# Decay rows of the state space heads through a scratch tensor in device memory, products in pairs, three of four causal blocks, folded norms

## The reference

```python
def hybrid_layer(...):
    h = rms_norm(x, norm1_w); proj = h @ w_in
    q, k, v, z, xbc, dt_raw = split(proj)
    q, k = rms_norm(q), rms_norm(k)                # 8 heads of 128
    attn = moba_attention(q, k, v)                 # 256 positions are one block: plain causal attention
    xs, bm, cm = split(silu(causal_dwconv(xbc)))
    y = ssd_chunked_scan(xs, softplus(dt_raw + dt_bias), -exp(a_log), bm, cm)   # 16 heads of 64
    y = rms_norm((y + d_skip * xs) * silu(z))      # 2 groups of 512 channels
    x = x + concat([attn, y]) @ w_out
    return x + (silu(u_gate) * u_val) @ w_down     # feed-forward, 5632 wide, with a convolution
def hybrid_layer_2(...):
    # modulation by c @ w_ada, dilated attention of 8 heads, retention of 4 heads in two directions
    o = o * rsqrt(mean(o * o) + eps)               # over the 256 channels of each retention head
```

## Time and profile before

| | us |
|---|---|
| time, median of 3 runs | 1633.7 (1627.95 to 1634.38) |
| the profiled execution's own time | 1634.53 |
| its span, first to last instruction | 1632.9 |
| PE busy with matmuls | 1586.1 (97%) |
| PE loading weights (overlaps) | 1557.8 (95%) |
| DVE busy | 1161.2 (71%) |
| ACT busy | 812.0 (50%) |
| mean granted PE clock | 0.990 |

### The profile page before, as it was taken

How to read it: one execution, slowest core, us unless ns; L and a number is a source line. 1 busy time by engine, 2 the same in 40 slices (tenths; PEclk the granted TensorE clock), 3 DMA queues, 4 the chain that set the end, 5 groups by cost and what they waited for, 6 DMA issues and landing times.

```text
span 1632.9 us, 33515 instructions
## 1 busy us (share of the span) xinstructions
PE 1586.1 (97%) x13230; PEld 1557.8 (95%) x13230; DVE 1161.2 (71%) x1359; ACT 812.0 (50%) x985; POOL 28.6 (2%) x54
## 2 busy tenths in 40 slices
PE   7999999999999999999999999999799999999998
PEld 7998899989999999999999999999799999999997
DVE  7676677775778888888888888666674554664754
ACT  6445355544564544545445454444455644445553
POOL 0000000000000000000000000000000000000000
PEclk9999999999999999999999999999989999999998
DMA  9453344455559777787777875555455555455451
GB/s 348 140 180 130 129 144 153 146 191 181 183 181 346 272 267 285 262 314 261 264 298 267 304 272 199 190 180 187 135 194 194 194 194 173 137 171 172 162 155 78
DMA packets 85186, 336.15 MB, mean 206 GB/s; under 512 B 9456, under 2 KB 9712, under 8 KB 78704
## 3 DMA queue, kind: packets, MB, share of 16 engines
q1 hardware_dynamic: 77328, 281.05, 50.2%
q0 software_dynamic: 7056, 51.38, 8.6%
q10 hardware_dynamic: 720, 2.52, 0.4%
HBM read 332.82 MB, written 2.10 MB: 205 GB/s over the span
## 4 chain that ended last, share of the span: by engine, by line
PE 72%; DVE 4%; issue 2%; ACT 1%; POOLq 0%; DVEq 0%; ACTq 0%
PE PS L1182 23%; PE PS L1184 23%; PE PS L1186 23%; DVE ada_w L996 1%; DVE wlo L627 1%; ACT whi L273 1%; PE PS L1317 1%; DVE UV L950 1%; PE PS L1284 1%; PE PS L1463 0%; PE PS L1303 0%; DVE X L643 0%; PE PS L1453 0%; PE PS L1471 0%; PE PS L1227 0%
## 5 line engine op out<-in xcount | busy, mean ns | idle before, releaser
L1182 PE MATMUL PS<-gh,whi 128*128 128x256 f32 x3504 | 992.4, 283 | 12.2 <-DVE wlo L627 10.4
L1184 PE MATMUL PS<-gl,whi 128*128 128x256 f32 x3504 | 977.9, 279 | 0.0
L1186 PE MATMUL PS<-gh,wlo 128*128 128x256 f32 x3504 | 977.6, 279 | 0.0
L627 DVE TENSOR_TENSOR wlo<-raw,whi 128x1024 fp32r<-128x1024 f32 x528 | 643.9, 1223 | 405.9 <-ACT whi L273 404.9
L273 ACT ACTIVATE whi<-raw 128x1024 fp32r<-128x1024 f32 x528 | 556.9, 1059 | 697.8 <-PE PS L1186 695.2
L1182 PEld LDWEIGHTS PS<-gh,whi 128*128 128x128 f32 x3504 | 663.5, 189 | 19.5 <-issue 17.4
L1184 PEld LDWEIGHTS PS<-gl,whi 128*128 128x128 f32 x3504 | 662.5, 189 | 2.8 <-issue 1.9
L1186 PEld LDWEIGHTS PS<-gh,wlo 128*128 128x128 f32 x3504 | 664.5, 190 | 0.0
L1182 PE MATMUL PS<-ah,whi 128*128 128x256 f32 x688 | 194.5, 283 | 10.8 <-DVE UV L950 7.2
L1184 PE MATMUL PS<-al,whi 128*128 128x256 f32 x688 | 193.0, 281 | 0.0
L1186 PE MATMUL PS<-ah,wlo 128*128 128x256 f32 x688 | 192.9, 280 | 0.0
(11 more groups left out here) (212 smaller groups left out, 845.6 us busy)
## 6 DMA issues: line engine op xcount, KB each, us to landing
raw<-weights SPq DMA_DIRECT2D x528, 512.0 KB, 3.5
ada_w<-w_ada POOLq DMA_DIRECT2D x48, 1024.0 KB, 5.9
outT<-X SPq DMA_DIRECT2D x4, 512.0 KB, 2.8
X<-xT SPq DMA_DIRECT2D x3, 512.0 KB, 8.7
c<-const ACTq DMA_DIRECT2D x1, 1536.0 KB, 7.1
c_act<-c_rows POOLq DMA_DIRECT2D x1, 1024.0 KB, 9.8
X<-xT SPq DMA_DIRECT2D x2, 256.0 KB, 5.2
prm<-params ACTq DMA_DIRECT2D x1, 276.5 KB, 4.6
```

Of the source, the lines that this page charges most:

```text
L627: dve.tensor_tensor(wlo[:, j % SPLIT, :], raw[:, j, :], whi[:, j % SPLIT, :].bitcast(F32), ALU.subtract).then_inc(s_lo, 1)
L1182: pe.matmul(out[:, t, :], whi[:, b, w], hi[:, kt, :], start=first and half == 0 and (apart or t % 2 == 0), stop=False, skip_group_check=True)
L1184: pe.matmul(out[:, t, :], whi[:, b, w], lo[:, kt, :], start=False, stop=False, skip_group_check=True)
L1186: mm = pe.matmul(out[:, t, :], wlo[:, b, w], hi[:, kt, :], start=False, stop=last and half == 1, skip_group_check=True)
```

## The change

Decay rows go through device memory. ACT writes three copies of the rows to `ACUM`, POOL stores them to a scratch tensor `rows` (16 x 384), waits, and loads them back to every partition (128 x 6144 floats, 3.1 MB) into a full-size `EM`, which lies where `ada_w` and `c_act` will be; so `c_act` is now loaded after the first projection:

```diff
         def _(pool):
-            pool.wait_ge(s_gh, DT)
+            pool.wait_ge(s_at, 2)
+            pool.dma_start(rows, ACUM[...]).then_inc(s_rows, 16)
+            pool.wait_ge(s_rows, 16)
+            pool.dma_start(EM[...], rows.rearrange("h l -> (h l)").unsqueeze(0).to_broadcast([P, SSM_HEADS * 3 * P])
+                           ).then_inc(s_r, 16)
+            pool.wait_ge(s_evac, G_OUT + 2)
             pool.dma_start(c_act[:, :], c_rows).then_inc(s_crow, 16)
-            pool.wait_ge(s_evac, G_OUT + 2)
# ACT
                 if n == 19:
-                    act.activation(small[0:16, 256:512], PS[0:16, 7, S:2 * S], ACT.Copy).then_inc(s_at, 1)
+                    act.activation(ACUM[:, 0:2, :], PS[0:16, 7, S:2 * S]..., ACT.Copy).then_inc(s_at, 1)
+                    act.activation(ACUM[:, 2, :], PS[0:16, 7, S + P:2 * S], ACT.Copy).then_inc(s_at, 1)
-                if n == 32:
+                if n == IN_SLOTS + 27:
                     act.activation(c_act[:, :], c_act[:, :], ACT.Silu).then_inc(s_c, 1)
-                if 35 <= n < 35 + SSM_HEADS:
+                if 35 <= n < 35 + SSM_HEADS and n % 2:
+                    j = (n - 35) // 2
+                    act.wait_ge(s_e, 6 * j + 6)
+                    act.activation(EM[:, 2 * j:2 * j + 2, :, :], EM[:, 2 * j:2 * j + 2, :, :], ACT.Exp)
```

DVE's `decay(h)` stays in slot 34+h, but works in place in `EM`; the exponential and `weigh` now take two heads at once, in the slot of the second one's `decay`. PE drops the 16 row matmuls and takes two heads in every second slot:

```diff
             def decay(h):
-                dve.wait_ge(s_r, h + 1)
                 if h == 0:
+                    dve.wait_ge(s_r, 16)
-                    dve.tensor_scalar(EM[:, h % 3, k, :], PS[:, 4 + h % 2, lo:lo + P], NB[:, k, h:h + 1], 0.0, ...)
+                    dve.tensor_scalar(EM[:, h, k, :], EM[:, h, k, :], NB[:, k, h:h + 1], 0.0, ...)
+            def weigh(j):
+                dve.wait_ge(s_ex, j + 1)
+                pair = EM[:, 2 * j:2 * j + 2, :, :]
+                dve.tensor_tensor(pair, pair, CB[:, j // 4, :, :].unsqueeze(1).to_broadcast([P, 2, 3, P]), ALU.mult)
-                if 35 <= n < 35 + SSM_HEADS:
-                    weigh(n - 35)
+                if 35 <= n < 35 + SSM_HEADS and n % 2:
+                    weigh((n - 35) // 2)
# PE
-                if 34 <= n < 34 + SSM_HEADS:
-                    pe.matmul(PS[:, 4 + h % 2, 0:S], ident[0:16, h:h + 1].to_broadcast([16, P]), small[0:16, 256:512], ...)
-                if 37 <= n < 37 + SSM_HEADS:      # one head: two matmuls, 256 and 128 columns
+                if 37 <= n < 37 + SSM_HEADS and n % 2:
+                    j = (n - 37) // 2
+                    pe.wait_ge(s_m, j + 1)
+                    for c in range(2):
+                        for q in (2 * j, 2 * j + 1):
+                            lo = 64 * (q % 2)
+                            out = PS[lo:lo + 64, 6 + j % 2, P * c:S]
+                            em = EM[:, q, 0:2, :] if c == 0 else EM[:, q, 2, :]
+                            mm = pe.matmul(out, XD[:, c, 64 * q:64 * q + 64], em, start=(c == 0), stop=(c == 1), ...)
+                    mm.then_inc(s_y, 1)
```

The sums for the norms are folded on DVE first; the state space norm moves one slot later on PE, ACT and DVE:

```diff
-                if n in (56, 57):
-                    ssm_norm(n - 56)
+                if n in (54, 55):
+                    dve.wait_ge(s_ysq, n - 53)
+                    y = SQY[n - 54]
+                    link(dve.tensor_tensor(y[:, 0:2, :], y[:, 0:2, :], y[:, 2:4, :], ALU.add))
+                    dve.tensor_tensor(y[:, 0, :], y[:, 0, :], y[:, 1, :], ALU.add).then_inc(s_yf, 1)
+                if n in (57, 58):
+                    ssm_norm(n - 57)
# PE, state space norm: 4 matmuls a group at n = 55, 56 become 1 at n = 56, 57
-                    for t in range(4):
-                        mm = pe.matmul(PS[:, 6 + g, 0:S], ones, SQY[g][:, t, :], start=(t == 0), stop=(t == 3))
+                    pe.matmul(PS[:, 6 + g, 0:S], ones, SQY[g][:, 0, :], start=True, stop=True).then_inc(s_ysum, 1)
# retention, layer 2: DVE adds the two tiles at step 3, PE sums one at step 5
+                        dve.tensor_tensor(both[:, 0, :], both[:, 0, :], both[:, 1, :], ALU.add).then_inc(s_rf, 1)
```

Attention of layer 1 leaves the masked block out everywhere: scores of 128 and 256 columns in place of 2 x 256, scale and mask over 384 in place of 512, the maximum as two instructions (128 and 256) in place of one over 512, exponential and division over 128 and 256, three transposes in place of four, a copy of 384, and 256 and 128 columns with v:

```diff
-                        mm = pe.matmul(PS[:, 4, S * c:S * c + S], q[:, P * c:P * c + P], k, start=True, stop=True)
+                        at, keys = (S * c, S) if layer else (P * c, P + P * c)
+                        mm = pe.matmul(PS[:, 4, at:at + keys], q[:, P * c:P * c + P], k[:, 0:keys], start=True, stop=True)
+                        for b in range(2 if layer else c + 1):     # transposes
+                        first = 0 if layer else P * b
+                        mm = pe.matmul(PS[:, 6, first:S], VS[:, h % 2, b, :], PTS[:, h % 2, b, 0:S - first], ...)
```

More of the change, by code:

```diff
@@ L75, with build @@
 ADA_STEP = 6
-def build(nc, xT, weights, w_dt, w_ada, c_rows, params, const1, const2, outT):
+def build(nc, xT, weights, w_dt, w_ada, c_rows, params, const1, const2, rows, outT):
     ctx = ExitStack()
@@ L120, in build @@
         U, o = place("U", [P, 12, S + 3], offset=o)
-        mask, o = place("mask", [P, 2, S], offset=o)
+        mask, o = place("mask", [P, 3 * P], offset=o)
         conv_acc, _ = place("conv_acc", [P, 4, S], offset=o)
@@ L126, in build @@
         assert o <= nc.sbuf_usable_end, (o, nc.sbuf_usable_end)
+        EM, e = place("EM", [P, SSM_HEADS, 3, P], offset=ada_at)
+        assert e <= area
+        ACUM, _ = place("ACUM", [SSM_HEADS, 3, P], offset=area + 1024 * Q0)
         SQX1, _ = place("SQX1", [P, 2, 4, S], offset=area + 1024 * Q0)
@@ L175, in spread, with seen @@
             return PS[:, 2 * late_par[k - 2] + 1, 0:S]
+        def seen(h, c):
+            flat = SB1[:, h % 2, :, :].rearrange("p c d -> p (c d)")
+            return flat[:, P:3 * P] if c else flat[:, 0:P]
         def acc_tiles(par):
@@ L379, in attention @@
                         k = 2 * (h % 2) + b
-                        act.activation(SB[:, h % 2, b, :], SB[:, h % 2, b, :], ACT.Exp, bias=small[:, k:k + 1],
+                        rows = SB[:, h % 2, b, :] if layer else seen(h, b)
+                        act.activation(rows, rows, ACT.Exp, bias=small[:, k:k + 1],
                                        accum_out=small[:, 4 + k:5 + k]).then_inc(s_exp, 1)
@@ L385, in attention @@
                         act.wait_ge(s_pv, H - 1)
[L386 to L387 removed]
+                    if layer:
+                        act.activation(PTS[:, h % 2, :, :], PS[:, 5, :].rearrange("p (c d) -> p c d", c=2),
+                                       ACT.Copy).then_inc(s_pts, 1)
+                    else:
+                        act.activation(PTS[:, h % 2, :, :].rearrange("p c d -> p (c d)")[:, 0:3 * P], PS[:, 5, 0:3 * P],
+                                       ACT.Copy).then_inc(s_pts, 1)
                 if step == 5 and layer == 0:
@@ L853, in attention @@
                     for b in range(2):
-                        dve.tensor_scalar(SB[:, h % 2, b, :], SB[:, h % 2, b, :], small[:, 8 + k + b:9 + k + b], None,
-                                          ALU.mult).then_inc(s_pn, 1)
+                        rows = SB[:, h % 2, b, :] if layer else seen(h, b)
+                        dve.tensor_scalar(rows, rows, small[:, 8 + k + b:9 + k + b], None, ALU.mult).then_inc(s_pn, 1)
                 if step == 5 and layer:
@@ L1120, in slot2 @@
                         retained(r)
+                    if step == 3:
+                        dve.wait_ge(s_rsq, r + 1)
+                        both = SQR[:, r % 2, :, :]
+                        dve.tensor_tensor(both[:, 0, :], both[:, 0, :], both[:, 1, :], ALU.add).then_inc(s_rf, 1)
                     if step == 5:
@@ L1316, in attention @@
                     for b in range(2):
-                        mm = pe.matmul(PS[:, 6, 0:S], VS[:, h % 2, b, :], PTS[:, h % 2, b, :],
+                        first = 0 if layer else P * b
+                        mm = pe.matmul(PS[:, 6, first:S], VS[:, h % 2, b, :], PTS[:, h % 2, b, 0:S - first],
                                        start=(b == 0), stop=(b == 1))
@@ L1370, in slot1 @@
                     pe.matmul(PS[:, 6 + g, S:S + P], bm[:, P:S], cm[:, P:S], start=True, stop=True).then_inc(s_cb, 1)
-                if 34 <= n < 34 + SSM_HEADS:
-                    h = n - 34
-                    pe.wait_ge(s_xd, 16)
-                    if h >= 2:
-                        pe.wait_ge(s_e, 3 * h - 3)
-                    pe.matmul(PS[:, 4 + h % 2, 0:S], ident[0:16, h:h + 1].to_broadcast([16, P]), small[0:16, 256:512],
-                              start=True, stop=True).then_inc(s_r, 1)
@@ L1466, in slot2 @@
                     if step == 5:
-                        pe.wait_ge(s_rsq, r + 1)
+                        pe.wait_ge(s_rf, r + 1)
                         if r:
                             pe.wait_ge(s_rrt, r)
-                        for e in range(2):
-                            mm = pe.matmul(PS[:, 7, 0:S], ones, SQR[:, r % 2, e, :], start=(e == 0), stop=(e == 1))
-                        mm.then_inc(s_rsum, 1)
+                        pe.matmul(PS[:, 7, 0:S], ones, SQR[:, r % 2, 0, :], start=True, stop=True).then_inc(s_rsum, 1)
```

84 lines of the change are left out of this document (42 added, 42 removed).

## The result

| | before | changed |
|---|---|---|
| median, us (runs) | 1630.83 (1624.9 to 1634.38, 4) | 1602.41 (1599.52 to 1610.16, 4) |
| ratio, 95% interval | | 0.9836 [0.9803, 0.9868] |
| profiled execution, its span | 1634.53, 1632.9 | 1599.52, 1597.9 |
| mean granted clock | 0.990 | 0.988 |

By the ratio the change is worth 1.64%, or 26.8 us of 1630.8 (21.5 to 32.1); the two medians are 28.4 apart. The direction was forecast, the size was not: 1616 was the forecast, and the time lies 3.6 us under the lower end of the range. The two profiled executions are 35.0 us apart because the one of before took longer than all four of its timed runs and the one of after was the fastest of its four.

What follows compares the result with a forecast made beforehand. PE was taken as the bound, busy 1586.1 of 1632.9 us. Streaming gains of 22.0 less 1.6, 1.5, 0.3 and 0.4 made 18.2 us, so 1634.5 - 18.2 = 1616.3 us; range 1606 to 1628.

Steps and rivals of the forecast that it cites:

- Rows, 10.7: Slots 34 to 49: removing the row matmuls from PE's path gains 10.7 us, with the replacing transfer hidden.
- Head products in pairs, 2.7: State space heads: 8 pairs at 1.64 us, 13.1 in place of 15.8, gain 2.7; bounds gain 7.9 to loss 1.3.
- Rival 1: Head product pairs: the two column halves overlap, a pair costs 0.99, 5.2 us more gained, time 1612; chance 20%.
- Folds and the masked block, 8.6: Norm sums, attention scores, products with v and transposes: fewer or shorter PE instructions gain 8.6 us; covering DVE adds cost 0.
- the pace was an unknown of its own: All PE stretches: matmuls run at 0.1175 or 0.1132 us, cause unknown; 7 us allowed either way.
- Given back, 3.8: Slots 34 to 91: longer waits and clock loss give back 1.6, 1.5, 0.3 and 0.4 us.
- The half clock behind slot 68, 1.5: After slot 68's transposes wait 2.9 us, PE's clock falls to 1.2 in place of 2.4 GHz, losing 1.5 us.
- Losses in slots 87 to 91: Same DVE chain as before, PE comes 0.2 us earlier to it: 0.3 us lost.
- The base: Forecast subtracted from the profiled execution's 1634.5 us, 0.8 above the median of the runs it used.
- 2, the pace turns: Long PE stretches: 100 to 150 us more run at the slow pace, giving 1625 us; chance 15%.
- 3, DVE piles up: Slots 34 to 70: larger delay and late weight splits cost 3 to 7 us more, giving 1621; chance 10%.
- 4, the broadcast is late: Row load to all partitions: gain gone if it takes over 62 us; 1676 us at 30 GB/s; chance 5%.

Runs made afterwards that it cites:

- e10: Kernel before, with only the decay rows stored and read back to all partitions in place of their matmuls: 1624.36 us, ratio 0.9925 to the kernel before.
- e3: Changed kernel with the 16 row matmuls back on PE, without store and broadcast: 1613.93 us, ratio 0.9887 to the kernel before.
- e4: Changed kernel without the folds of the state space and retention norms: 1611.80 us, ratio 0.9861 to the kernel before.
- e5: Changed kernel with all four blocks of layer 1's attention computed again, the masked one included: 1610.60 us, ratio 0.9876 to the kernel before.
- e8: Changed kernel, unaltered, timed and profiled again: 1602.89 us, ratio 0.9829 to the kernel before.
- e1: Changed kernel with the four matmuls of a pair ordered head by head: 1609.66 us, ratio 0.9842 to the kernel before.
- e6: Changed kernel with the state space norm a slot earlier, folds kept where they were: 1598.65 us, ratio 0.9832 to the kernel before.

## Why the prediction was wrong

The forecast was 1616.3 and the median 1602.4, 13.9 us lower. By stretches, in us gained:

| units | forecast | measured | what it holds |
|---|---|---|---|
| 33 to 60 | 15.6 | 20.65 | rows, pairs, the state space norm |
| 60 to 98 | 0.9 | 2.97 | attention, less waits and clock |
| 98 to 127 | 0 | 3.27 | nothing that was changed but the last product with v |
| retention | 1.7 | 1.26 | its folded sums |
| together | 18.2 | 28.15 | |

The other 3.7 of the 13.9 are the base. By the prediction's own steps:

1. **Rows, 10.7: right.** 10.76 in e10, and 11.59 in e3 where 11.8 less 0.3 were due. The transfer cost nothing; it landed in 11.2 us, where 31 had been worked out from the earlier trace rows.
2. **Head products in pairs, 2.7: the step that failed.** A pair was priced at 1.64, "if the four matmuls follow each other and the going over is paid once". They don't follow each other: the pair costs 1.00, and the gain is 15.8 - 8 x 1.01 = 7.7, **5.0 more**, all of the excess between units 33 and 60. Rival 1 had this price, and was given 20%; its time, 1612, would have been 9.6 too high all the same. I had leaned on the fact that no row showed two halves side by side, and on each fp32 matmul being two instructions of one half; neither is evidence against the overlap. The Trainium skill, page "TensorEngine Tiling (Array Packing)", sections Key Properties and Theoretical Speedup, says that tiles work independently and that 64 columns can give up to 2x. The traces agree with the first: 1.00 for one head and for two in two halves. Of the second, the whole pair gains 1.66 to 1.00; without the 0.34 of going over it would be 1.3 to 0.65.
3. **Folds and the masked block, 8.6: right in the prices, with a term left out.** Norms gave 4.0 of 4.3 (e4), the attention's pieces about 4.0 of 4.3 (e5). But with the masked block 3.9 us of slow pace go too, in units 76 to 82 and 98 to 127, which the sum put at nothing: the pace was an unknown of its own, 7 us either way. e5 shows that it comes with the block; why, no run shows.
4. **Given back, 3.8: the second miss.** Slot 67 waits 0.13 (forecast 0.6), slot 68 0.77 more than before, and slots 43 and 49 lose 0.15 each. Slots 87 to 91 lose 0.1: they are 0.37 shorter (20.11 and 19.74), where the smaller blocks are worth 0.5. That is 1.3 in all, and 1.5 in e8. Two parts of the reasoning fell:
   - *The half clock behind slot 68, 1.5.* The wait was 2.66 where I had 2.9, and the clock stayed at 1.00, in e8 too. In e1 the same wait of 2.67 was followed by 0.50, and there the price was right: from the transposes of slot 68 to those of slot 70 it is 9.12 us against 7.48. And in e10 the wait of 1.89, behind which the kernel before kept its full clock, was followed by 0.50. So the size was right and the occurrence isn't decided by the length of the wait.
   - *Losses in slots 87 to 91 were added.* They aren't additive, as the wait that moves shows.
5. **The base.** I subtracted from the profiled 1634.5; the median of before in the result's runs was 1630.8. That alone is 3.7 of the 13.9.

So the gain was forecast 10.0 us too small, and with the base that makes 13.7 of 13.9. That the rest is so small is luck: units 127 to 381 alone differed by 8.2 us between two executions.

**The wait that moves.** PE's timeline from the scores of slot 89 to the transposes of slot 90, of the changed kernel, of the same kernel again, and of e1, with the idle time before and its releaser in brackets:

```profile
311.06 1.62 PE L1320 MATMUL PS<-QKVZ 128*128 128x128 f32 x4 [2.74 <-DVE SB L870]
317.45 0.38 PE L1332 MATMUL PS<-cst,QKVZ 128*128 128x128 f32 x2
317.66 0.49 PE L1341 MATMUL PS<-cst,SB 128*128 128x128 f32 x3
```

```profile
308.44 1.62 PE L1320 MATMUL PS<-QKVZ 128*128 128x128 f32 x4 [2.74 <-DVE SB L870]
313.33 0.38 PE L1332 MATMUL PS<-cst,QKVZ 128*128 128x128 f32 x2
314.97 0.44 PE L1341 MATMUL PS<-cst,SB 128*128 128x128 f32 x2 [1.26 <-DVE SB L881]
```

```profile
313.57 0.89 PE L1320 MATMUL PS<-QKVZ 128*128 128x128 f32 x4 [2.73 <-DVE SB L870]
...
320.10 0.90 PE L1341 MATMUL PS<-cst,SB 128*128 128x128 f32 x3 [2.68 <-DVE SB L881]
```

The distances are 6.60, 6.53 and 6.53 us, whether PE ran at half clock throughout and then didn't wait, in part and waited 1.26, or at full clock and waited 2.68. DVE's scale, mask and division decide when the transposes may start; a slow PE only shortens its wait. The half clock that I priced at 1.2 to 1.5 from the earlier trace rows costs 0.07 there. (In e1 the second wait was followed by a fall of its own, and that one cost: units 82 to 98 took 61.85 in place of 60.63.) Behind slot 68 no wait follows in slot 70, and there it costs 1.64 when it comes (e1).

**Slots 57 to 70.** The delay came nearly as worked out. PE's matmuls for the q/k norm of slot 60 start at 209.66, DVE's first inversion at 213.39, 3.7 later (forecast 4.0, before 2.5):

```profile
209.66 1.02 PE L1437 MATMUL PS<-PTS,cst 128*128 128x512 f32 x2
```

```profile
213.39 3.35 DVE L840 RECIPROCAL SB<-SB 128x512 f32<-128x512 f32 x1
```

In e6 and in e4 that distance is back to what it was before (2.5; from the last unit matmul of slot 60 it is 2.61 in all three, 3.85 in the changed kernel), and in both the wait of slot 68 is 1.84: that this delay lengthens it is shown. That the norm's later slot alone makes the delay isn't: in e4 the norm kept that slot, and PE comes later to slot 60 in both (by 2.3 in e4 and 1.0 in e6, counted from unit 33).

*The other rivals.* 2, the pace turns: it is real, and went the other way, in part by chance (units 127 to 381, e8) and in part with the change (3.9 us, e5); its price of 9 us also took 220 us of slow stretch, where its condition says 100 to 150. 3, DVE piles up: no late split; refuted. 4, the broadcast is late: refuted by 30 us of room.

## What to carry to other kernels

Two products with 64 output columns each belong in the two column halves, in one slot: here the second one was free, and the order of their matmuls didn't matter. Before adding up waits and clock losses of one stretch, ask whether another engine's chain sets its end: losses of the waiting engine in front of a wait that remains are not losses. And subtract from the median of before, not from the one profiled execution; where the same sequence can run at two paces, compare distances between fixed places rather than spans: they show what repeats to a hundredth of a microsecond and where chance begins, and they also showed an effect of the change, in slots that it doesn't touch, that no price of a piece holds.

## What was not expected of the hardware

- **Column halves.** Two fp32 products of 64 output columns: 1.00 us in different halves of one bank, in either order, 1.66 in the same half of two banks; one alone 1.00.
- **Two paces.** Unit matmuls of 128x256 start every 0.113 or every 0.1175 us for stretches of over 100 us at a granted clock of 1.00. With one exception in e10, the pace changes only where two neighbouring matmuls stand further apart than either pace, after a small piece, a wait, or as little as 0.03 us. Between two executions of the same program it differs by some 9 us in all; yet units 98 to 127 were slow in all three traces with the masked block and fast in all nine without it.
- **The same wait with and without a fall of the clock.** After 2.66 to 2.67 us of idle in slot 68 the granted clock was 1.00 in the changed kernel and its repetition and 0.50 in e1 (first line: the window behind slot 68 in e1; second: behind slot 89 in e1, after 2.73 us), and after 1.89 us there it was 1.00 before and 0.50 in e10.

```profile
241.00:244.00 3.00, 3.00 (x15) 3.00 (x15) 2.97 (x5) 1.42 (x5) 0.00 (x0) 0.50 0.32 81
314.00:317.00 3.00, 3.00 (x27) 2.95 (x26) 3.00 (x3) 1.94 (x5) 0.83 (x2) 1.00 0.87 280
```

- **A load to all partitions.** 3 MB read from the same 24 KB landed in 11.2 and 11.8 us beside the weight stream, faster by bytes than the 1 MB of distinct data in the earlier trace rows.
